# Eight early features of the first chunk instead of six in a split-product feed-forward kernel

## The reference, cut to what matters

```python
def _swiglu(h, w_gate, w_up, w_down):
    return (jax.nn.silu(h @ w_gate) * (h @ w_up)) @ w_down

mod = jax.nn.silu(c) @ p['w_mod'][l] + p['b_mod'][l]      # 9 vectors of 1024
h = _rmsnorm(x, ng[0]) * (1.0 + sc1) + sh1
x = x + g1 * 0.5 * _swiglu(h, gate[l, 0], up[l, 0], down[l, 0])
# attention and recurrent group, with sh2, sc2, g2
h = _rmsnorm(x, ng[2]) * (1.0 + sc3) + sh3
x = x + g3 * 0.5 * _swiglu(h, gate[l, 1], up[l, 1], down[l, 1])
```

## Time and profile before

| | |
|---|---|
| median of three runs | 2294.21 us |
| the profiled execution | 2290.62 us |
| its span, first to last instruction | 2288.8 us |
| mean granted TensorE clock | 0.991 |
| TensorE busy | 2201.2 us, 96% |
| DVE busy | 1549.0 us, 68% |
| ACT busy | 817.2 us, 36% |

### The profile page before, as it was taken

The page is one execution under the profiler, slowest core; times in us unless marked ns, Lnnn a source line. Parts: engine busy times, 40 slices in busy tenths (PEclk is TensorE's granted clock), DMA queues, the critical chain, the costliest instruction groups (busy, mean ns, idle before and its releaser), DMA issues.

```text
span 2288.8 us, 34204 instructions
## 1 busy us (share of the span) xinstructions
PE 2201.2 (96%) x13240; PEld 2098.3 (92%) x13240; DVE 1549.0 (68%) x2604; ACT 817.2 (36%) x1458; POOL 27.1 (1%) x34
## 2 busy tenths in 40 slices
PE   5989999999999999999989999999999999999997
PEld 4989999999999988869967769999999999999996
DVE  6977776778888674766468884686545456756556
ACT  5522323234111234563146562444323233421122
POOL 0000000000000000000010030000000000000000
PEclk9999999999999999999989999999999999999998
DMA  7333233334524312012001010222212123431312
GB/s 288 131 104 137 99 132 103 123 128 152 196 77 164 126 57 91 1 38 68 23 24 34 30 40 20 73 93 79 77 66 77 66 77 109 141 133 49 104 49 83
DMA packets 82145, 209.53 MB, mean 92 GB/s; under 512 B 9840, under 2 KB 36336, under 8 KB 82032
## 3 DMA queue, kind: packets, MB, share of 16 engines
q1 hardware_dynamic: 82032, 207.99, 26.6%
HBM read 172.04 MB, written 35.92 MB: 91 GB/s over the span
## 4 chain that ended last, share of the span: by engine, by line
PE 90%; DVE 6%; ACT 2%; issue 1%; DMA 0%; DVEq 0%; ACTq 0%
PE ps L696 18%; PE ps L698 18%; PE ps L697 18%; PE ps L771 9%; PE ps L772 9%; PE ps L773 9%; PE ps L999 4%; PE ps L1028 2%; PE ps L938 2%; PE ps L1014 1%; DVE sb_nmx L2204 1%; DVE sb_hL L1702 1%; DVE sb_tmp L1711 1%; PE ps L720 1%; DVE sb_x L1728 0%
## 5 line engine op out<-in xcount | busy, mean ns | idle before, releaser
L696 PE MATMUL ps<-sb_hH,sb_wH 128*128 128x384 f32 x1664 | 562.7, 338 | 7.6 <-DVE sb_hL L1702 4.7
L698 PE MATMUL ps<-sb_hH,sb_wL 128*128 128x384 f32 x1664 | 557.3, 335 | 0.0
L697 PE MATMUL ps<-sb_hL,sb_wH 128*128 128x384 f32 x1664 | 557.2, 335 | 0.0
L696 PEld LDWEIGHTS ps<-sb_hH,sb_wH 128*128 128x128 f32 x1664 | 313.4, 188 | 14.7 <-DVE sb_hL L1702 5.4
L697 PEld LDWEIGHTS ps<-sb_hL,sb_wH 128*128 128x128 f32 x1664 | 313.4, 188 | 1.2 <-issue 0.3
L698 PEld LDWEIGHTS ps<-sb_hH,sb_wL 128*128 128x128 f32 x1664 | 313.4, 188 | 0.0
L2006 DVE SCALAR_TENSOR_TENSOR sb_x<-ps,sb_mod,sb_x 128x384 f32<-128x384 f32 (+2 forms) x384 | 186.4, 514 | 173.1 <-PE ps L698 167.8
L771 PE MATMUL ps<-sb_hH,sb_wH 128*128 128x384 f32 x704 | 235.4, 334 | 1.4 <-DVE sb_tmp L1834 1.1
L773 PE MATMUL ps<-sb_hH,sb_wL 128*128 128x384 f32 x704 | 235.2, 334 | 0.0
L772 PE MATMUL ps<-sb_hL,sb_wH 128*128 128x384 f32 x704 | 235.1, 334 | 0.0
L1178 ACT ACTIVATE sb_wH<-sb_wide 128x512 fp32r<-128x512 f32 x176 | 110.9, 633 | 227.8 <-DVE sb_wide L1756 222.8
(11 more groups left out here) (241 smaller groups left out, 3588.9 us busy)
## 6 DMA issues: line engine op xcount, KB each, us to landing
sb_raw<-in_w_gate SPq DMA_DIRECT2D x56, 512.0 KB, 3.5
sb_raw<-in_w_up SPq DMA_DIRECT2D x56, 512.0 KB, 3.6
sb_raw<-in_w_mod SPq DMA_DIRECT2D x56, 512.0 KB, 3.6
hidden<-sb_tmp SPq DMA_DIRECT2D x132, 192.0 KB, 2.2
sb_hid_raw<-hidden SPq DMA_DIRECT2D x40, 576.0 KB, 6.1
sb_raw<-in_w_dn SPq DMA_DIRECT2D x80, 256.0 KB, 2.7
sb_stage<-in_w_mod SPq DMA_DIRECT2D x4, 2048.0 KB, 15.5
sb_raw<-in_w_in SPq DMA_DIRECT2D x16, 512.0 KB, 4.1
```

Of the source, the lines that this page charges most:

```text
L696: pe.matmul(o, wH, xH, start=begin, stop=False)
L697: pe.matmul(o, wH, xL, start=False, stop=False)
L698: return pe.matmul(o, wL, xH, start=False, stop=end)
```

## The change

`EARLY` becomes 8, so `MAIN` becomes 14, in both feed-forwards. The operands B11, T2, T1 and T3 are cast and completed one behind each of the last four early features. `MID_MOD` becomes 11, so that seven blocks instead of six fall into the down projection; `down_step` now skips steps 19 to 23 instead of 16 to 23.

```diff
-EARLY = 6
+EARLY = 8
 MAIN = FT - EARLY
...
 MID_MOD = PRE + MAIN // 2
+MOD_PAUSE = 2 * KT + 3
...
 OP_ORDER = (B11, T2, T1, T3, B21, B22, T4)
+OPS_AT = {EARLY - 4: (B11,), EARLY - 3: (T2,), EARLY - 2: (T1,), EARLY - 1: (T3,)}
...
         def down_step(s):
-            n = s if s < 2 * KT else s - KT
-            if 2 * KT <= s < 3 * KT or not 0 <= n < 5 * (NB_MOD - MID_MOD):
+            n = s if s < MOD_PAUSE else s - (3 * KT - MOD_PAUSE)
+            if MOD_PAUSE <= s < 3 * KT or not 0 <= n < 5 * (NB_MOD - MID_MOD):
                 return None, None
             return MID_MOD + n // 5, n % 5
...
                         early_cast(z, 1, w + 2)
-                    if w == EARLY - 2:
-                        op_cast(z, B11)
-                        op_cast(z, T2)
+                    for b in OPS_AT.get(w, ()):
+                        op_cast(z, b)
                 for q, o in enumerate((S1, S2, S3, S4)):
                     sum_cast(o, 4 * FT * z + q + 1)
-                    if q == 1:
-                        op_cast(z, T1)
-                op_cast(z, T3)
                 op_cast(z, B21)
...
                     if w < KT // 2:
                         op_front(z, w)
-                    elif w == EARLY - 2:
-                        op_low(z, B11)
-                        op_low(z, T2)
+                    for b in OPS_AT.get(w, ()):
+                        op_low(z, b)
                 for o in SUMS:
                     sum_of(o, 4 * FT * z + SUMS.index(o) + 1, (p_w[1], FT * z + EARLY))
                 sum_low(S1, 4 * FT * z + 1)
                 sum_low(S2, 4 * FT * z + 2)
-                op_low(z, T1)
                 sum_low(S3, 4 * FT * z + 3)
                 sum_low(S4, 4 * FT * z + 4)
-                op_low(z, T3)
                 op_low(z, B21)
```

## The result

The changed kernel takes 2297.81 us (median of 18 runs, 2296.09 to 2300.98), the kernel before 2293.31 us in the same comparison (18 runs, 2290.25 to 2300.38). The ratio is 1.0016, 95% interval [1.0009, 1.0024]: 3.7 us slower, between 2.1 and 5.5, which is within 0.3%. The forecast was 2297.0 us, +2.8. The profiled execution of the changed kernel took 2299.22 us around a span of 2297.4. That is 8.6 us over the span of before, more than the runs show, so not all of it belongs to the change.

What follows compares the result with a forecast made beforehand. The prediction took TensorE as the bound, busy 2201.2 of 2288.8 us. Its terms, -1.55 + 3.03 + 1.3 = +2.8 us, added to the median of 2294.21 us, gave 2297.0 us, range 2290 to 2303.

Steps and rivals of the forecast that it cites:

- Short group, +3.03 us: Down projection, steps 16 to 18: three modulation parts outrun the six banks, TensorE waits 0.89 and 2.14 us, cost 3.03 us.
- First wait, -1.55 us: First feed-forward's first combined feature: waits of 0.28 and 5.00 us become one of 4.0 us, gain 1.55 us.
- Operands B11, T2, T1, T3 move ... DVE then catches up: First combined feature: moving these operands earlier lets y_one start 0.15 us after product S2 instead of 1.70 us.
- Unchanged wait of 1.13 us at the second feature: First feed-forward, second combined feature: the 1.13 us wait stays, because the chain from up_two on is not touched.
- Clock, +1.3 us behind the second wait of the short group: Short group: the clock drops behind the new 2.14 us wait, nine matmuls at 0.32 instead of 0.173 us, cost 1.3 us.
- The clock behind the first wait, put at 0: First combined feature: the low clock behind the shortened wait of 4.0 us stays as before, cost 0.
- The second loading: Both feed-forwards: early features are loaded and split twice; TensorE hides the added transfers, casts and lows, cost 0, or 9.0 us exposed.
- no wait of TensorE in the early features at present: Early features: TensorE has no wait there now, used as the argument against an exposed added chain of 9.0 us.
- The banks hide the modulation parts: Rival: short-group parts cost nothing, only the 1.55 us gain and at most 1.3 more show, 2291.4 to 2292.7 us; chance 0.12.
- the short group in full: Rival: each of three modulation parts is paid fully, +8.6 us, 2302.8 us; chance 0.10 together with exposed second loading.
- All stalls go: Rival: all waits at the start of both feed-forwards vanish, 9.3 us, giving 2284.9 us; chance 0.03.
- The second loading shows: Rival: the added loading chain of 9.0 us is exposed, 2303 to 2306 us; chance 0.10 together with the fully paid short group.

Runs made afterwards that it cites:

- before_parts: Kernel before with only the three modulation parts moved into steps 16 to 18 of the short down group, six early features; 2297.08 us, ratio 1.0018.
- spread: Changed kernel with the three modulation parts in steps 16, 19 and 22 instead of 16, 17 and 18; 2294.9 us, ratio 1.0002 to the kernel before.
- square of four kernels: Six or eight early features, each with old or new operand places; first wait 5.00 (six, old), 4.98 (six, new), 3.92 (eight, old), 3.93 us (eight, new).
- old_ops: Changed kernel, eight early features, with operands B11, T2, T1 and T3 back in the places of before; 2297.12 us, ratio 1.0009 to the kernel before.
- six_new_ops: Kernel before, six early features, with B11 behind the fourth, T2 behind the fifth, T1 and T3 behind the sixth; 2295.85 us, ratio 1.0007.
- chain: Changed kernel with the low part of T4 moved behind up_two and the modulation part behind the third sum; 2293.06 us, ratio 0.9996 to the kernel before.
- pad: Kernel before with four added, unused memory-to-memory transfers of 512 KB ahead of the spills of x; 2295.61 us, ratio 1.0007.

## Why the prediction was right, and where it was not

The time came out 0.8 us from the forecast, and by the ratio 3.7 us against 2.8. The mechanism that decides the sign is the one forecast, but of the three terms one is right in mechanism and size, one in size alone, and one is absent, while others that were put at nothing are not. That the total came so close is partly luck.

*Short group, +3.03 us: right.* 24.96 became 28.02, +3.06, and `before_parts` and `spread` show it by putting it in and taking it out. The rows of DVE in the changed kernel follow the sum step by step:

```profile
669.07 1.79 DVE L2001 SCALAR_TENSOR_TENSOR sb_x<-ps,sb_mod,sb_x 128x128 f32<-128x128 f32 x4 [0.21 <-DVE sb_rq L1811]
...
674.33 1.79 DVE L2001 SCALAR_TENSOR_TENSOR sb_x<-ps,sb_mod,sb_x 128x128 f32<-128x128 f32 x4 [0.22 <-DVE sb_rq L1811]
...
679.58 1.79 DVE L2001 SCALAR_TENSOR_TENSOR sb_x<-ps,sb_mod,sb_x 128x128 f32<-128x128 f32 x4 [0.21 <-DVE sb_rq L1811]
```

Their distance is 5.26 us, 5.25 were worked out from the earlier trace rows, and from the third on DVE gains on TensorE until DVE waits again at 693.30. The idle times read 0.71 and 1.88 where 0.89 and 2.14 were forecast; the group's length, which holds all of it, is the better measure.

*First wait, -1.55 us: right in size, wrong in its reason.* The failing step is "Operands B11, T2, T1, T3 move ... DVE then catches up". The square of four kernels shows that the move does nothing measurable: the two further features alone give the time (in `old_ops`, with the places of before, DVE idles 3.81 and 1.13 us before the last two hidden products). And it was not DVE alone that was late. Of the 1.70 us by which y_one came late before, DVE's own work makes 1.20, to 109.66; the last 0.50, in the earlier trace rows as "[0.50 <-ACT sb_tmp L1213]", is a wait for ScalarE, which has to copy a result for y_one and does so behind its casts of B21 and B22. ACT's timeline of the kernel before:

```profile
105.24 4.15 ACT L1197 ACTIVATE sb_r2H<-sb_last_raw,sb_mod 128x384 fp32r<-128x384 f32 x8
109.29 0.47 ACT L1184 ACTIVATE sb_tmp<-ps 128x384 f32<-128x384 f32 x1
109.66 0.47 ACT L1213 ACTIVATE sb_tmp<-ps 128x384 f32<-128x384 f32 x1
```

In the first feed-forward ACT releases y_one in all seven traces with six features (0.50 us, 0.97 in `six_new_ops`), TensorE in all seven with eight. Once y_one is on time, the wait is the rest of the chain, as the prediction had it: 4.0 worked out, 3.93 measured. `chain` tested this the other way, by shortening the chain, and the waits of both feed-forwards went.

*Unchanged wait of 1.13 us at the second feature: wrong.* It is 0 and 0.38 us in the two traces of the changed kernel. The step "the chain from up_two on is not touched" left out TensorE's side: the slow matmuls ahead of that point hold TensorE back while DVE runs on. The wait moves so without any change: in `before_parts` and `pad`, whose code in these two features is that of before, it is 0.38 and 0.42 us behind 3.1 us of slow time, in the two traces of before 1.13 and 1.12 behind 2.0 and 2.3. Slow time and this wait read as two forms of one lateness: together 3.1 to 3.8 us in five traces with six features, 2.2 to 2.9 in four with eight.

*Clock, +1.3 us behind the second wait of the short group: wrong.* The granted clock stayed at 1.00 in the changed kernel, and 24 matmuls take 4.24 to 4.26 us behind the wait of 1.85 to 1.89 us in all five traces that have it. It was sized by one row, where 2.15 us ahead of 1484.84 is followed by a clock of 0.57. The kernel before, run again, has the same wait of 2.14 us at the same instruction, and the window of 3.7 us behind it, and a later one, read:

```profile
1490.19:1493.89 3.70, 3.56 (x17) 2.85 (x17) 3.66 (x11) 2.10 (x5) 0.00 (x0) 1.00 0.00 0
1496.20:1502.90 6.70, 6.23 (x24) 5.01 (x25) 2.36 (x5) 0.93 (x3) 0.00 (x0) 0.50 0.00 0
```

Over the fourteen traces the first window is at 0.57 to 0.60 in six and at 1.00 in eight, for the same 2.14 or 2.15 us. The second row shows that a clock of 1.00 right behind the wait isn't the end of it: TensorE has two or three shorter waits (0.4 to 1.0 us) in the 9 us that follow, and in four of the eight the lower level comes 6 to 9 us after the long wait. In the other four it doesn't come. The clock behind the first wait, put at 0, was 2.0 and 2.3 us of slow time and restart in two traces before and 2.9 and 2.5 in two after. That is no effect of the change: `before_parts` and `pad`, with the wait of before, have 3.1, and `spread`, with the wait and the places of the changed kernel, has 1.8. The stretch at the lower level is 120.1 to 123.5 us in the first trace of before, 117.2 to 123.9 in the second, 133.9 to 140.7 in the first of the changed kernel and 134.5 to 137.9 in `spread`; how much of it is slow matmuls depends on where it begins beside the wait. The Trainium skill (TensorE: Matmul & The Clock Gate, on the HAM clock gate) says of the monitor's window that it is free-running; the traces agree, with these six and eight, and with the wait of 2.57 or 2.59 us that had a clock of 1.00 behind it in one kernel and 0.50 in another. By that rule the prediction itself had worked out +1.5 us for the executions without the low clock, and it took the row instead.

*Put at nothing, and not nothing.* The second loading: tail features of the first feed-forward wait 0.23 us in one trace and 0.53 + 0.43 in the other; over the seven traces with eight features it is 0 to 0.96 us, 0.3 on the mean, and in none of the seven with six features is there a wait. The 0.23 us follow a sum that waited for its weights; VectorE's timeline of the changed kernel:

```profile
510.01 0.69 DVE L1754 TENSOR_TENSOR sb_wide<-sb_raw 128x512 f32<-128x512 f32 x1 [1.88 <-DMA sb_raw<-in_w_up]
```

The added early features hold no wait, but the prediction's "no wait of TensorE in the early features at present" and "No wait in the eight early features" are wrong as they stand. The first early features wait in every trace, with either number, and the windows of the earlier trace rows leave them out; that costs the sum nothing. Of the kernel before:

```profile
43.42 0.45 PE L696 MATMUL ps<-sb_hH,sb_wH 128*128 128x384 f32 x1 [2.69 <-DVE sb_hL L1702]
...
61.78 0.41 PE L696 MATMUL ps<-sb_hH,sb_wH 128*128 128x384 f32 x1 [1.08 <-ACT sb_tmp L1184]
```

The late store of `out_k`: 1.6 us of TensorE's wait.

The sum as measured, from two traces of either kernel: -1.7 for the first two stretches, +3.1 short group, +0.6 tail features, +1.6 store, 3.6 us; the runs say 3.7 (2.1 to 5.5). The 0.90 us at the collection are left out, because such a wait comes and goes with either number of features. Forecast and time agree partly because the missing terms (+2.2) stand in for one that was not there (+1.3). The account isn't closed either: from the gate projection to the mixing of the output the seven traces with six features take 465.0 to 470.1 us, 467.2 on the mean, the seven with eight 468.2 to 473.0, 470.6 on the mean. TensorE's idle time there is 27.0 and 28.3 us on the mean, which is about what the store costs; the rest of the 3.4 us goes with the time at the lower clock, 22.4 and 28.8 us. Why it is longer is not known.

*The rivals.* "The banks hide the modulation parts" and "the short group in full" both fell with the 3.06 us. "All stalls go" fell for this change; `chain` shows what it takes. "The second loading shows" fell in its size: at most 0.96 us of waits in a trace, not 9.0.

## What to carry to other kernels

When an engine stops for the end of a chain on another engine, list what stands in that chain, in order, and take out what the waiting engine doesn't need yet; giving the chain's engine more time ahead of it only helps until its start is on time (5.28 to 3.93 us here, whereas two moved operations took the wait away and 4 us of the whole). Extra work for a nearly full engine belongs one piece per several steps, spread over what the banks can buffer. And a forecast within a microsecond is no proof of its terms: put each in and take it out.

## What the runs showed that I had not expected

- The clock behind a wait is not set by the wait's length. Slow time and restart behind the first feature's wait: 1.8, 1.8, 2.5 and 2.9 us after 3.9 us; 2.0, 2.3, 3.1, 3.1 and 3.3 us after 5.0 us. Behind 1.9 us in the short group it never fell (five traces), behind 2.15 us at the start of the second feed-forward in six traces of fourteen at once and in four 6 to 9 us later, behind 2.5 to 2.6 us at the second combined feature once in five.
- The same 256 KB store lands in 2.5 to 2.7 us in all seven traces of kernels with six early features and in 3.8 to 4.3 in all seven with eight, whether or not other loads are issued behind it or four more ahead. A 16 KB packet of the queue called "instruction" falls into the store in the seven slow ones and in none of the others.
- Unchanged code of some 470 us differs by up to 8 us between traces (464.97 to 473.00), in granted clock and in waits for the softmax. TensorE's clock is at the lower level for 44.3 us in one trace of the kernel before and for 68.3 us in the other. One pair of traces can't carry a difference of 4 us; local windows can, which here repeat within 0.6 us (44.09 to 44.61, 46.21 to 46.54).
